# Two MLPs in a fused block: the first matrix takes x without the norm's factor, and its results are scaled afterwards

## The reference, cut to what matters

```python
def rmsnorm(x, g):
    x32 = x.astype(jnp.float32)
    y = x32 * lax.rsqrt(jnp.mean(x32 * x32, axis=-1, keepdims=True) + EPS)
    return (y * g.astype(jnp.float32)).astype(x.dtype)

def modulate(h, shift, scale):
    return h * (1 + scale) + shift

def sq_relu_mlp(h, w1, w2):
    return jnp.square(jax.nn.relu(h @ w1)) @ w2
...
        x = x + g2 * sq_relu_mlp(modulate(rmsnorm(x, norm_g[l, 1]), sh2, s2), w_ff1[l], w_ff2[l])
```

## Time and profile before

| | |
|---|---|
| time, median of 3 runs | 1676.1 us (1674.89 to 1676.59) |
| the profiled execution | 1674.75 us, span in the profile 1673.5 us |
| mean granted TensorE clock | 0.945 |
| TensorE busy | 1420.0 us (85%) |
| VectorE busy | 1189.5 us (71%) |
| ScalarE busy | 725.0 us (43%) |
| GpSimd busy | 336.5 us (20%) |
| first MLP, from its norm to the last residual add | about 234 to 431 us |
| second MLP | about 579 to 779 us |

### The profile page before, as it was taken

One profiled execution on the slowest core, in us unless ns is written; L12 is line 12 of the kernel. 1 busy time (PEld: TensorE's weight loads), 2 busy tenths in 40 slices (PEclk: granted clock), 3 DMA queues, 4 the chain that ended last, 5 costly groups with the idle time before them and its releaser, 6 DMA issues.

```text
span 1673.5 us, 20648 instructions
## 1 busy us (share of the span) xinstructions
PE 1420.0 (85%) x7544; PEld 1053.6 (63%) x7544; DVE 1189.5 (71%) x2335; ACT 725.0 (43%) x1631; POOL 336.5 (20%) x313
## 2 busy tenths in 40 slices
PE   7898789999898789998998987997777777777776
PEld 2777679999897689998977875553332222222222
DVE  1678678777798777777566479777777787777644
ACT  2534445555557555555234354434333343333322
POOL 1100010000100100002001014365444444444340
PEclk9899899999999899999899698999999999999998
DMA  9575338888540567784332049999999999999995
GB/s 394 199 279 213 114 127 326 306 324 304 200 152 1 201 231 289 289 292 159 120 132 101 26 144 397 419 418 420 420 420 420 420 421 420 421 420 420 420 420 218
DMA packets 65909, 477.67 MB, mean 285 GB/s; under 512 B 7312, under 2 KB 7312, under 8 KB 8336
## 3 DMA queue, kind: packets, MB, share of 16 engines
q0 software_dynamic: 36864, 268.45, 38.7%
q1 hardware_dynamic: 28800, 206.85, 33.8%
q10 hardware_dynamic: 144, 1.05, 0.2%
HBM read 475.27 MB, written 1.05 MB: 285 GB/s over the span
## 4 chain that ended last, share of the span: by engine, by line
PE 39%; DMA 27%; DVE 19%; ACT 5%; issue 3%; POOL 1%; POOLq 0%; ACTq 0%; DVEq 0%
DMA ring<-in_uv,crow 16%; PE ps L1878 7%; DMA row_h<-in_uv,crow 5%; PE ps L1510 5%; PE ps L1511 5%; PE ps L1512 5%; DMA row_x<-in_uv,crow 4%; DVE HID L757 4%; PE ps L1757 4%; PE ps L1760 4%; PE ps L1759 4%; DVE WB L457 3%; DVE ring L442 3%; ACT WB L1042 2%; DMA ring<-in_um 1%
## 5 line engine op out<-in xcount | busy, mean ns | idle before, releaser
L457 DVE TENSOR_TENSOR WB<-ring,WB 128x1024 fp32r<-128x1024 f32 x232 | 284.8, 1228 | 118.6 <-ACT WB L1042 116.6
L1042 ACT ACTIVATE WB<-ring 128x1024 fp32r<-128x1024 f32 x232 | 243.4, 1051 | 133.3 <-PE ps L1760 87.4
L1510 PE MATMUL ps<-hH,WB 128*128 128x256 f32 x920 | 271.4, 295 | 15.0 <-DVE WB L457 9.1
L1878 PE MATMUL ps<-ring,P 128*128 128x512 f32 x448 | 213.7, 622 | 68.6 <-ACT P L1359 67.2
L1511 PE MATMUL ps<-hL,WB 128*128 128x256 f32 x920 | 264.3, 287 | 0.0
L1512 PE MATMUL ps<-hH,WB 128*128 128x256 f32 x920 | 264.0, 287 | 0.0
L1878 PEld LDWEIGHTS ps<-ring,P 128*128 128x128 f32 x448 | 84.0, 197 | 192.7 <-ACT P L1359 103.6
L976 DVE CUSTOM_DVE_ANT_0 ring<-ring,cT 128x1024 f32<-128x1024 f32 x112 | 136.4, 1226 | 81.3 <-DMA ring<-in_uv,crow 80.2
L1510 PEld LDWEIGHTS ps<-hH,WB 128*128 128x128 f32 x920 | 180.5, 196 | 21.2 <-DVE WB L457 12.3
L1349 ACT ACTIVATE On<-On 128x2 f32<-128x2 f32 x128 | 26.0, 203 | 378.1 <-DVE On L976 378.0
L1511 PEld LDWEIGHTS ps<-hL,WB 128*128 128x128 f32 x920 | 180.6, 196 | 2.2 <-issue 2.2
(11 more groups left out here) (278 smaller groups left out, 2768.9 us busy)
## 6 DMA issues: line engine op xcount, KB each, us to landing
ring<-in_stream SPq DMA_DIRECT2D x116, 1024.0 KB, 5.0
ring<-in_um SPq DMA_DIRECT2D x64, 1024.0 KB, 7.0
ring<-in_wm SPq DMA_DIRECT2D x8, 1024.0 KB, 9.8
bias<-in_bias SPq DMA_DIRECT2D x2, 2048.0 KB, 12.1
ring<-in_uv,crow POOLq DMA_INDIRECT x112, 27.7
xT<-in_xT ACTq DMA_DIRECT2D x1, 1024.0 KB, 6.0
cT<-in_cxT SPq DMA_DIRECT2D x1, 1024.0 KB, 9.1
crow<-in_crow SPq DMA_DIRECT2D x2, 512.0 KB, 10.3
```

The costliest lines, as they stand in the source:

```text
L457: ve.tensor_tensor(unit_dst(j, 1), unit_src(j), f(unit_dst(j, 0)), ALU.subtract).then_inc(s_lo, 1)
L1042: se.activation(unit_dst(j, 0), unit_src(j), ACT.Copy).then_inc(s_hi, 1)
L1510: te.matmul(o, wh[:, c], hi[:, kt, :], start=(kt == 0), stop=False)
L1878: mm = te.matmul(ps[4 + 2 * n + q][:, :], diag[:, g % 8, :], row_ap[row_of[g]][:, 1024 + q * 512:1536 + q * 512], start=(g % 128 == 0), st ...
```

## The change

The norm's rstd is not applied to x any more. `z_begin`, `z_hi` and `z_lo` make high and low part of x·a as soon as a channel group of x is there, and columns 256 and 257 of the same tiles hold the shift's high and low part. ff1's matmuls have 258 columns. The results are multiplied on VectorE by rstd (the two last columns by 1.0) into a buffer `ev`, and ScalarE's relu reads `ev` with column 256 as its bias. So ff1's PSUM banks are emptied by VectorE instead of ScalarE. The unit f2 writes to bank 3 and is left out of the two banks' turn. The sum of squares on TensorE is made inside `rows2`, ahead of channel group 6. ScalarE makes the high part of a unit one tile earlier in the program's order (`ahead(... + 1)`). In the residual loops in front of the MLPs, `unit` comes ahead of the residual add. The shares of the modulation steps are 0.3 for ff1 and 1.1 or 0.9 for ff2.

```diff
-        share = {"w_in": 1.6, "w_out": 0.9, "ff1_0": 0.7, "ff2_0": 0.7, "pw2": 1, "ff1_1": 0.6, "ff2_1": 0.6,
+        share = {"w_in": 1.6, "w_out": 0.9, "ff1_0": 0.3, "ff2_0": 1.1, "pw2": 1, "ff1_1": 0.3, "ff2_1": 0.9,
...
+        third = {("ff1_0", 0, 2, 0): 3, ("ff1_1", 0, 2, 0): 3}
...
-            if w == "iw" or w in ("w_out", "w_out2"):
+            if w == "iw" or w in ("w_out", "w_out2", "ff1_0", "ff1_1"):
                 return "V"
```

VectorE, the new functions, the loop in front of the first MLP, and ff1's part of `mlp`:

```diff
+            def z_begin(n, i_ab, layer, g):
+                have_mod(layer, 4)
+                z_scale.then_inc(ve.scalar_tensor_tensor(out=ab[:, i_ab, :], in0=M[:, layer, 32:40], scalar=1.0, in1=g,
+                                                         op0=ALU.add, op1=ALU.mult), n)
+
+            def z_lo(n, kt, i_ab, layer):
+                V.wait_ge(*n_hi[n, kt])
+                if kt == 0:
+                    V.then_inc(ve.tensor_tensor(zL[:, :, 256:258], M[:, layer, 24:32].unsqueeze(2).broadcast_to([128, 8, 2]),
+                                                f(zH[:, :, 256:258]), ALU.subtract))
+                    V.wait_ge(*z_scale[n])
+                h_in.then_inc(ve.scalar_tensor_tensor(out=hL[:, kt, :], in0=xT[:, kt, :], scalar=ab[:, i_ab, kt:kt + 1],
+                                                      in1=f(hH[:, kt, :]), op0=ALU.mult, op1=ALU.subtract), (n, kt))
...
+            z_begin("mlp0", 1, 0, col["ng"][:, 8:16])
             for u in range(4):
+                unit(unit_at["w_out", 1, u])
                 into_x(1, u)
-                unit(unit_at["w_out", 1, u])
+                for kt in (2 * u, 2 * u + 1):
+                    z_lo("mlp0", kt, 1, 0)
...
                             unit(first[f"ff1_{l}", s] + u)
+                            if (s, u) == (0, 0):
+                                rstd(n)
+                            name, i = (f"ff1_{l}", s, u, 0), 4 * s + u
+                            V.wait_ge(*dense[name])
+                            if i >= 2:
+                                V.wait_ge(*relu_r[l, (i - 2) // 4, (i - 2) % 4])
+                            elif l:
+                                V.wait_ge(*relu_r[0, 7, 3])
+                            out_v.then_inc(ve.tensor_tensor(ev[:, i % 2, :], row_bank(name)[:, 0:258], r, ALU.mult), name)
                             tail()
...
             for b in range(2):
                 for u in range(4):
                     kt = 4 * b + u
+                    unit(first["pw2", b] + u)
                     V.wait_ge(*out_a["pw2", b, u, 0])
                     x_done.then_inc(ve.tensor_tensor(xT[:, kt, :], xT[:, kt, :], ptmp[:, kt, :], ALU.add), ("pw2", kt))
-                    unit(first["pw2", b] + u)
+                    z_lo("mlp1", kt, 3, 1)
```

ScalarE:

```diff
+            def z_hi(n, kt, i_ab, layer, last):
+                S.wait_ge(*x_ready(n, kt))
+                if kt == 0:
+                    S.wait_ge(*z_scale[n])
+                    S.wait_ge(*dense[last])
+                    S.then_inc(se.activation(zH[:, :, 256:258], M[:, layer, 24:32].unsqueeze(2).broadcast_to([128, 8, 2]), ACT.Copy))
+                n_hi.then_inc(se.activation(hH[:, kt, :], xT[:, kt, :], ACT.Copy, scale=ab[:, i_ab, kt:kt + 1]), (n, kt))
...
                 if u == 2:
                     sqrt_next()
                 for kt in (2 * u, 2 * u + 1):
+                    z_hi("mlp0", kt, 1, 0, ("w_in", 0, 3, 0))
+                for kt in (2 * u, 2 * u + 1):
                     square("mlp0", kt)
...
-                            ahead(first[f"ff1_{l}", s] + u)
-                            name = (f"ff1_{l}", s, u, 0)
+                            ahead(first[f"ff1_{l}", s] + u + 1)
+                            name, i = (f"ff1_{l}", s, u, 0), 4 * s + u
                             if s >= 2:
                                 S.wait_ge(*relu_l[l, s - 2, u])
                             r = relu[:, s % 2, u, :]
-                            copy_out(name, r, row_bank(name)[:, 0:256], ACT.Relu)
+                            S.wait_ge(*out_v[name])
+                            relu_r.then_inc(se.activation(r, ev[:, i % 2, 0:256], ACT.Relu, bias=ev[:, i % 2, 256:257]), (l, s, u))
                             tail()
```

TensorE:

```diff
                 for kt in range(8):
+                    if kt == 6 and norm:
+                        mean_of_sum(norm)
                     T.wait_ge(*ready(kt))
...
-                                rows2(i, [(f"ff1_{l}", 0, 0, 0), (f"ff1_{l}", 0, 1, 0)], normed(n), (hH, hL))
+                                rows2(i, [(f"ff1_{l}", 0, 0, 0), (f"ff1_{l}", 0, 1, 0)], normed(n), (zH, zL), 258, n)
```

More of the change, by code:

```diff
@@ L205, in program @@
                 new = [(name, b, u, o) for o in range(2 if (name, b) == ("w_in", 3) else 1)]
-                row_tiles += new
+                row_tiles += [x for x in new if x not in third]
             elif name == "w_out":
@@ L222, in row_bank @@
         def row_bank(name):
-            return ps[row_at[name] % 2]
+            return ps[third[name] if name in third else row_at[name] % 2]
         def emptied_by(name):
             w, b, u = name[:3] if len(name) > 2 else (name[0], 0, 0)
-            if w == "iw" or w in ("w_out", "w_out2"):
+            if w == "iw" or w in ("w_out", "w_out2", "ff1_0", "ff1_1"):
                 return "V"
@@ L233, in emptied_by @@
                 return "AV"[u % 2]
-            if (w, b) in (("w_in", 1), ("w_in2", 6)) or w in ("ff1_0", "ff1_1", "pw2"):
+            if (w, b) in (("w_in", 1), ("w_in2", 6)) or w == "pw2":
                 return "VA"[w != "w_in2" or u != 1]
@@ L298, in program @@
         hs = ["x0", "ctx", "mlp0", "conv", "mlp1", "b2", "ffn"]
-        n_sc = Steps(sem("dve_scaled"), [(n, k) for n in hs for k in range(8)])
+        n_sc = Steps(sem("dve_scaled"), [(n, k) for n in ("x0", "ctx", "conv", "b2", "ffn") for k in range(8)])
         n_hi = Steps(sem("act_h_hi"), [(n, k) for n in hs for k in range(8)])
@@ L328, in program @@
         cat_h, cat_l = Steps(sem("act_cat"), cats), Steps(sem("dve_cat"), cats)
+        relu_r = Steps(sem("act_relu"), [(l, s, m) for l in range(2) for s in range(8) for m in range(4)])
+        z_scale = Steps(sem("dve_z_scale"), ["mlp0", "mlp1"])
         relu_a = Steps(sem("act_relu_square"), [(l, s, m) for l in range(2) for s in range(8) for m in range(4)])
@@ L720, in mlp @@
                         for u in range(4):
-                            if s < 8:
-                                unit(first[f"ff2_{l}", s - 1] + u)
+                            unit(first[f"ff2_{l}", s - 1] + u)
                             if u == 0:
@@ L732, in mlp @@
                                         scalar=M[:, l, 40 + kt:41 + kt], in1=xT[:, kt, :], op0=ALU.mult, op1=ALU.add), (n, kt))
-                                unit(first[f"ff2_{l}", s - 1] + u)
-            mlp(0, 1, col["ng"][:, 8:16])
+            mlp(0)
             have_mod(1, 2)
@@ L806, in dve @@
                     ve.tensor_tensor(XL[:, k, :], yc[:, k, :], f(XH[:, k, :]), ALU.subtract).then_inc(s_yl, 1)
+            z_begin("mlp1", 3, 1, col["ng"][:, 24:32])
             for b in range(2):
@@ L1193, in act @@
                 for kt in (2 * u, 2 * u + 1):
+                    z_hi("mlp0", kt, 1, 0, ("w_in", 0, 3, 0))
+                for kt in (2 * u, 2 * u + 1):
                     square("mlp0", kt)
-            root("mlp0")
             def mlp(l):
                 n = f"mlp{l}"
-                norm(n, M[:, l, 24:32])
+                ahead(first[f"ff1_{l}", 0])
+                root(n)
                 tails = []
@@ L1275, in act @@
                         sqrt_next()
+                    z_hi("mlp1", kt, 3, 1, ("pw1", 3, 3, 0))
                     square("mlp1", kt)
-            root("mlp1")
             mlp(1)
@@ L1496, in mean_of_sum, with rows @@
                 moment.then_inc(mm, n)
-            def rows(i, name, ready, hl, half=0):
+            def rows(i, name, ready, hl, width=256):
                 hi, lo = hl
@@ L1503, in rows @@
                 T.wait_ge(s_hi, i + 1)
-                if row_at[name] >= 2:
+                if name not in third and row_at[name] >= 2:
                     T.wait_ge(*empty(row_tiles[row_at[name] - 2]))
-                o = row_bank(name)[:, 0:256]
+                o = row_bank(name)[:, 0:width]
                 for kt in range(8):
@@ L1513, in rows, with rows2 @@
                 dense.then_inc(mm, name)
-            def rows2(i, names, ready, hl):
+            def rows2(i, names, ready, hl, width=256, norm=None):
                 hi, lo = hl
```

27 lines of the change are left out of this document (14 added, 13 removed).

## The result

The changed kernel takes 1690.0 us (median of 4 runs, 1687.8 to 1696.3) against 1675.5 of the kernel before on the same chip (1673.9 to 1676.6): ratio 1.0088, 95% interval 1.0071 to 1.0104. It is slower by 14.5 us. The forecast was 1685 within 1675 to 1693.

A forecast was written before the change was run, and what follows sets the result against it. TensorE's matmuls bound the steady part, and the change acts at the MLPs' starts: first MLP 5.8, second 2.4, columns 1.3, sum 9.5 us on the profiled 1674.75; with 1.35 for the median, 1685 us, range 1675 to 1693.

The forecast's parts named there:

- one left at nothing: Unit calls moved ahead of the last residual adds at the MLPs' ends: no cost, covered by TensorE's tile.
- Front of the first MLP: Residual adds before the first MLP: f0 at about 242.0 instead of 240.18, TensorE idle about 6 us ahead of it.
- The loop: VectorE and ScalarE queues before the first MLP wait on each other: 4.6 us a turn against the tile's 2.87.
- Rival (a): Front of the MLPs overlaps if the loop turns in under 2.87 us: faster, 1666 us; chance 0.13.
- Opening: First MLP up to the first ff2 tile, f8: f8 at 274.7 against 268.82, +5.8 us including the front.
- the stall: First MLP's opening: TensorE waits 5 us at f5, whose bank VectorE's multiply 3 must empty first.
- R: Start of VectorE's reciprocal in the MLP's opening, 2.4 us behind the sum of squares' start: 250.8 in the first MLP.
- the second stall: First MLP's opening: multiply 5, which f7's bank waits for, comes late at R + 20.9, another 1.0 us.
- Second MLP: Loop through pw2's eight tiles, then the opening: f0 at 584.8 instead of 584.48, f8 at 617.5 against 615.1, +2.4 us.
- Two more columns: ff1's 1536 matmuls get 2 columns at 0.42 ns each: +1.3 us, tiles of ff1 20 ns longer.
- Steady part: Body of the first MLP: VectorE needs 21.5 us per eight tiles against TensorE's 23.0, so it fits at 94%.
- rival (b): VectorE becomes the bound through waits for steps' rows or longer multiplies: 1692 for the first MLP alone, 1699 both; chance 0.16.

The follow-up runs named there:

- e3: Changed kernel with ScalarE's high part of the next unit ahead of z_hi and the squares in both residual loops before the MLPs: 1685.3 us, ratio to before 1.0064.
- e4: Changed kernel with no modulation steps beside f0 to f7 of either MLP, the steps made up beside later units: 1693.1 us, ratio to before 1.0109.
- e5: Changed kernel with the MLPs' modulation steps set, none beside ff1's units and ff2's last block: 1692.8 us, ratio to before 1.0100.
- e1: Changed kernel with the residual add again ahead of the next unit's low part in each MLP's last ff2 block: 1683.4 us, ratio to before 1.0046.
- e2: Kernel before with only the next unit's low part moved ahead of the residual add in each MLP's last ff2 block: 1680.1 us, ratio 1.0033.
- e8: Changed kernel with the old shares of modulation steps, 0.7 and 0.6 beside both matrices: 1692.8 us, ratio to before 1.0107.
- e6: Kernel before with the hand-set plan of modulation steps from e5: 1662.5 us, ratio 0.9914.
- e11: Kernel before with e6's plan and one step more beside pw2's units (2, 2, 2, 2, 1), an odd count: 1672.8 us, ratio 0.9989.
- e7: Changed kernel with e5's plan, the old order in the last ff2 block and ScalarE's high part first: 1681.2 us, ratio to before 1.0032.
- e10: e7 with one step fewer beside pw2's units (2, 2, 2, 1, 1), an even count: 1660.2 us, ratio to before 0.9916.

## Why the prediction was right, and where it was not

The direction was right and the time lies in the range (1685 forecast, 1690 measured), but the change cost half as much again as the sum had it, 14.5 us against 9.5. Two of its four terms came as worked out or nearly so, one was too large, and one left at nothing was 7.7. That fronts, openings and bodies together measured just the 9.5 us of the sum (2.1 + 6.1 + 1.3) is partly luck, as the paragraphs below show.

**Front of the first MLP: right.** The loop closed. The adds stand 4.66, 4.82 and 4.79 us apart (4.6 predicted), from the second pair on:

```profile
231.16 0.87 DVE L677 SCALAR_TENSOR_TENSOR xT<-ps,M,xT 128x256 f32<-128x256 f32 x2
234.68 1.23 DVE L463 TENSOR_TENSOR WB<-ring,WB 128x1024 fp32r<-128x1024 f32 x1 [0.99 <-ACT WB L1073]
235.82 0.87 DVE L677 SCALAR_TENSOR_TENSOR xT<-ps,M,xT 128x256 f32<-128x256 f32 x2
239.23 1.48 DVE L463 TENSOR_TENSOR WB<-ring,WB 128x1024 fp32r<-128x1024 f32 x1 [1.08 <-ACT WB L1073]
240.64 0.86 DVE L677 SCALAR_TENSOR_TENSOR xT<-ps,M,xT 128x256 f32<-128x256 f32 x2
```

The front is 2.0 us longer (1.8 predicted); TensorE idles 6.6 us ahead of f0 (6). e3 shows the cause: ScalarE's order. Rival (a) needed a turn under 2.87, and e3's 3.94 shows that reordering alone doesn't give it. The starts forecast, f0 at 242 and f8 at 274.7, came as 246.55 and 279.82, of which 4.4 us lie ahead of the loop.

**Opening: the stall right, its price too low.** VectorE's queue from the reciprocal to multiply 3, then f5 on TensorE:

```profile
254.43 1.75 DVE L475 RECIPROCAL rr<-rr 128x256 f32<-128x256 f32 x1 [4.37 <-ACT rr L1084]
...
263.22 0.42 DVE L747 TENSOR_TENSOR ev<-ps,rr 128x258 f32<-128x258 f32 x1
...
266.00 1.28 DVE L448 CUSTOM_DVE_ANT_0 ring<-ring,crow,cols 128x1024 f32<-128x1024 f32 x1
...
267.21 1.28 DVE L448 CUSTOM_DVE_ANT_0 ring<-ring,crow,cols 128x1024 f32<-128x1024 f32 x1
...
268.41 0.42 DVE L747 TENSOR_TENSOR ev<-ps,rr 128x258 f32<-128x258 f32 x1
```

```profile
268.98 0.55 PE L1552 MATMUL ps<-hH,WB 128*128 128x258 f32 x1 [4.91 <-DVE ev L747]
269.33 0.42 PE L1553 MATMUL ps<-hL,WB 128*128 128x258 f32 x1
...
273.42 0.42 PE L1554 MATMUL ps<-hH,WB 128*128 128x258 f32 x1
...
273.82 0.28 PE L1553 MATMUL ps<-hL,WB 128*128 128x258 f32 x1
```

R is 254.43 and f5 starts 14.55 us behind it (14.2 predicted), after 4.91 us idle (5). What the sum lacked is the clock: from 268.98 to 273.63 matmuls come 0.215 us apart, the level of 1.2 GHz, which costs 2.0 us. I had counted this behind f0's wait, not behind this one. It swallowed the second stall (f7, 1.0). Behind f0's wait the lower clock lasted for 15 matmuls instead of the 21 that I had taken, so R came 7.9 us behind f0 instead of 8.8. That f0 to f8 is 33.3 against 32.7 predicted is therefore partly luck. e4 and e5 show the cause of the stall: without steps there, 26.2.

**Second MLP: right in kind.** Front +0.1 (+0.3 predicted), opening +1.5 (+2.1). I had f8 of the kernel before at 615.1, one tile behind f7; it came at 616.7, since f7's tile, after its wait of 3.00 us, ran partly at the lower clock. So the opening before was 1.6 longer than I had taken, and the opening after, 33.7, was 1.0 longer than the 32.7 of the sum: the two misses largely cancel.

**Two more columns: too large.** From start to start in TensorE's timeline, ff1's blocks of 96 matmuls in the second MLP take 11.53 us with 258 columns (median of six) and 11.52 in the kernel before, 11.534 and 11.520 before rounding. That is 0.15 ns a matmul and 0.2 us in all, not 1.3; a tile of ff1 is 3.5 ns longer, not 20. The slope between 256 and 512 columns doesn't hold for two.

**Steady part: nearly.** VectorE is busy 119.7 of the 146 us above and waits 18.6 for ScalarE, 95% together (94% predicted), and it fits. That the body's +1.2 us is near the 1.3 of the columns is luck. It is two waits at multiplies, in blocks of 12.13 and 12.21 us instead of 11.53, each behind a step that waited for rows (2.71 us and 1.19). The first step, and the matmul that waited for the multiply behind it:

```profile
340.81 1.29 DVE L448 CUSTOM_DVE_ANT_0 ring<-ring,crow,cols 128x1024 f32<-128x1024 f32 x1 [2.71 <-DMA ring<-in_um]
343.72 0.36 PE L1552 MATMUL ps<-hH,WB 128*128 128x258 f32 x1 [0.35 <-DVE ev L747]
```

This is rival (b)'s mechanism, in two blocks instead of all; e5's second MLP shows it in six blocks, up to 3.2 us each.

**The step that failed:** "At nothing: the `unit` calls moved ahead of the last residual adds (the low part is ready 2.3 us behind the tile before, the add waits for the tile)". This read one turn only. The low part needs ScalarE's high part, this stands behind squares, these behind the residual add of the turn before: the loop that I had worked out in front of the MLP, a second time. The ends are 3.9 us longer in each MLP, 7.7 of the 17.2 us; e1, which undoes this order alone, gives 7.4 of them back. The order by itself is 5.4 (e2, and the same ends in e8). The other 2.4 come with the modulation steps that the new shares put ahead of the block's first add, and with the lower clock behind the longer wait, a second thing that the forecast didn't have. With the old order these steps cost next to nothing (e1's ends are within 0.2 us of before).

**Open:** the medians differ by 14.5 us and the stages by 17.2. The parts outside the stages are 1210 to 1214 us in the profiles of eight kernels with the change and 1215 to 1219 in four without. Only the changed kernel's own profile, of its slowest run, has 1219, and 4.4 us of that lie ahead of the first MLP: `w_out`'s second half starts at 225.50 there and at 219.6 to 221.9 in the other eight. That stretch varies without the change too (221.1 to 225.9). Behind the second MLP the other eight are at most 3.4 us shorter than the kernel before. No experiment was made on either.

## What to carry to other kernels

When two engines hand work back and forth, write down for each loop turn what every queued instruction waits for, including the one of the turn before, and do so at every place where the order is changed: the swap that I had put at nothing made a turn of 3.6 us where a tile takes 2.87. Work that fills a queue (here the modulation steps) belongs where nothing that empties a PSUM bank stands close behind it: without the pairs ahead of the first multiplies an opening is 7 us shorter (e4), while single steps beside the later tiles of ff1 added under 1 us to a body (e8). Its count has to fit the transfers that feed it: one step more or less was worth 10 to 21 us (e6 to e11, e7 to e10). Before a structural change is judged, give the old kernel the same tuning: with the plan (and the two orders mended in the changed one) the kernels reach 1662 and 1660 us. Their ratios to the kernel before, 0.9914 and 0.9916, don't differ by more than their intervals, and in the MLPs' eight stages the old one is 1.9 us ahead (446.0 against 447.9). So no gain of the change itself is shown.

## What was not expected of the hardware

A tensor_tensor of VectorE with two SBUF inputs takes 1.77 us instead of 1.22 when a GpSimd add of 256 columns began just before it (e3, 233.32 and 233.37). In the changed kernel's loop, with the adds lying otherwise, it is 1.48. The other way round, an add that began 0.17 us behind a low part (e3, 230.16 and 229.99) takes 1.64 us, while the low part keeps its 1.22; an add alone takes 0.74. The add behind a low part in e3, then one alone in the changed kernel:

```profile
230.16 1.64 POOL L1459 TENSOR_TENSOR sq<-sq 128x256 f32<-128x256 f32 x1 [165.08 <-ACT sq L1078]
233.78 0.74 POOL L1458 TENSOR_TENSOR sq<-sq 128x256 f32<-128x256 f32 x1 [168.43 <-ACT sq L1078]
```

The Trainium skill (SBUF — State Buffer, SBUF: two separate sides) says that a VectorE instruction with two SBUF inputs and a GpSimd instruction that reads SBUF take a shared port pair exclusively for a whole instruction, and that the one that comes second is blocked. Both rows fit: each time the second to start is the longer one, by 0.55 and 0.90 us. No run took the adds away, so this is read from starts and durations only.

Two columns beyond 256 cost 0.15 ns a matmul, not the 0.84 of the slope to 512 columns.
